# First block: woven projections paced by a running balance over all steps of a phase, and value projections awaited at their first use

## What is computed

```python
proj = h_res @ w_in[l]
(fq, fk, fv, f_logit, sq, sk, sv, c_q, c_kv, k_rot, mq, gate) = split(proj)
out_fox = causal softmax attention(fq, fk, fv, forget gates)         # 4 heads of 64
out_sb  = stick-breaking attention(sq, sk, sv)                       # 4 heads of 64
out_mla = causal softmax attention(rms(c_q) @ w_q_up, rms(c_kv) @ w_kv_up, rope)
out_mem = softmax attention(mq, mem_n @ w_mem_kv[l])                 # 256 memory tokens
y = (concat(out_fox, out_sb, out_mla, out_mem) * silu(gate)) @ w_out[l]
h_res = layer_norm(ALPHA * h_res + y)
```

## Time and profile before

| | us |
|---|---|
| median of 3 runs (2819.11 to 2820.87) | 2819.47 |
| the profiled execution | 2825.36 |
| its span in the trace | 2823.5 |
| TensorE busy | 2645.2 |
| VectorE busy | 1071.4 |
| ScalarE busy | 697.2 |
| first block, layer 0, fox to mem | 136 to 376 |
| first block, layer 1, fox to mem | 545 to 785 |

### The profile page before, as it was taken

The page is one execution under the profiler, slowest core; times in us unless marked ns, Lnnn a source line. Parts: engine busy times, 40 slices in busy tenths (PEclk is TensorE's granted clock), DMA queues, the critical chain, the costliest instruction groups (busy, mean ns, idle before and its releaser), DMA issues. The chain is left out here.

```text
span 2823.5 us, 43376 instructions
## 1 busy us (share of the span) xinstructions
PE 2645.2 (94%) x17418; PEld 1388.3 (49%) x17418; DVE 1071.4 (38%) x2323; ACT 697.2 (25%) x1835; POOL 207.0 (7%) x253
## 2 busy tenths in 40 slices
PE   7999999999999989999999999988999989999897
PEld 3565654565645667555444444435765543322222
DVE  3023340023345854556112112245852552332234
ACT  2124321134322344422112111112442320000000
POOL 1100020000001001012100000001010010000000
PEclk9999999999999999999999999998999999999999
DMA  7243635343714001015999999981012249999996
GB/s 228 75 125 93 161 94 142 99 121 80 212 28 117 31 15 44 32 75 213 368 397 401 397 397 399 381 227 31 16 29 90 97 165 397 404 410 410 403 415 257
DMA packets 268622, 569.97 MB, mean 202 GB/s; under 512 B 12416, under 2 KB 203200, under 8 KB 219328
## 3 DMA queue, kind: packets, MB, share of 16 engines
q1 hardware_dynamic: 256512, 528.69, 51.3%
q0 software_dynamic: 11824, 39.18, 5.1%
q10 hardware_dynamic: 144, 0.14, 0.0%
HBM read 551.53 MB, written 16.42 MB: 201 GB/s over the span
## 5 line engine op out<-in xcount | busy, mean ns | idle before, releaser
L510 PE MATMUL ps<-turned,ring 128*128 128x512 f32 (+1 forms) x1056 | 406.6, 545 | 3.7 <-ACT turned L1745 3.0
L510 PEld LDWEIGHTS ps<-turned,ring 128*128 128x128 f32 x1056 | 201.8, 192 | 202.7 <-issue 191.0
L798 PE MATMUL ps<-ring,mixT 128*128 128x512 f32 x512 | 223.6, 594 | 0.8 <-DVE mixT L1961 0.8
L1391 ACT ACTIVATE work<-ps 128x512 f32<-128x512 f32 x32 | 19.1, 598 | 682.3 <-PE ps L1293 404.5
L2002 ACT ACTIVATE probsT<-ps 128x512 f32<-128x512 f32 (+3 forms) x280 | 120.2, 455 | 230.1 <-PE ps L626 145.7
L1935 DVE TENSOR_REDUCE col<-ps 128x1 f32<-128x256 f32 (+4 forms) x136 | 79.0, 581 | 257.6 <-PE ps L584 224.6
L584 PE MATMUL ps<-kz,qz 96*128 96x512 f32 (+3 forms) x320 | 134.9, 504 | 23.7 <-ACT probs_v L1989 10.8
L1989 ACT ACTIVATE probs_v<-ps,col 128x256 f32<-128x256 f32 (+5 forms) x216 | 136.3, 631 | 81.6 <-DVE col L1935 57.0
L533 PE MATMUL ps<-turned,ring 128*128 128x512 f32 (+1 forms) x352 | 154.6, 568 | 0.9 <-DMA ring<-in_w_in 0.9
L798 PEld LDWEIGHTS ps<-ring,mixT 128*128 128x128 f32 x512 | 95.9, 190 | 114.5 <-issue 113.2
L612 PE MATMUL ps<-const,probs_v 128*128 128x128 f32 x752 | 122.8, 281 | 17.1 <-DVE probs_v L1953 14.1
(11 more groups left out here) (325 smaller groups left out, 3844.7 us busy)
## 6 DMA issues: line engine op xcount, KB each, us to landing
ring<-in_w_gate SPq DMA_DIRECT2D x64, 1024.0 KB, 21.0
mixT<-in_w_up SPq DMA_DIRECT2D x64, 1024.0 KB, 15.0
ring<-in_w_mod SPq DMA_DIRECT2D x96, 512.0 KB, 5.5
ring<-in_w_up SPq DMA_DIRECT2D x48, 1024.0 KB, 20.9
ring<-in_w_in SPq DMA_DIRECT2D x82, 512.0 KB, 7.2
turned<-in_w_gate SPq DMA_DIRECT2D x32, 1024.0 KB, 19.3
mixcT<-in_w_down SPq DMA_DIRECT2D x32, 1024.0 KB, 17.6
probs_v<-in_w_down SPq DMA_DIRECT2D x32, 1024.0 KB, 18.5
```

The lines of the kernel that those rows point to most:

```text
L510: mm = nc.tensor.matmul(ps[:, b, 0:n], w[:, k, :], rhs[:, k, 0:n], start=(k == 0), stop=(k == KD - 1))
L798: mm = nc.tensor.matmul(ps[:, b, :], lhs[:, k, tl * P:(tl + 1) * P], w, start=(k == 0), stop=(k == KD - 1))
```

## The change

Three things. (1) `weave` keeps a balance: what a call leaves or overdraws is carried into the next (a saving up to one more call's budget, a debt in full), and the budgets fall from 2700, 3000 and 1900 a step to 2100, 2400 and 1450. (2) A bank taken by any job, not by woven ones alone, is known to `bank_free` with the step in which it was taken. (3) The waits for the evacuation of the last value projection (sv, mv, memv) move from the start of the phase that uses them to its first value product.

```diff
--- before.py
+++ after.py
@@ -295,6 +295,7 @@
                 pe.wait_ge(*emptied(bank_user[b]))
             bank_user[b] = job
             places[("job", job)] = b
+            closing[job] = now[0]
             return b
 
         def pe_busy(pe, n):
@@ -319,6 +320,7 @@
 
         closed = {}
         closing = {}
+        now = [(None, 0)]
 
         def bank_free(fill):
 
@@ -340,6 +342,7 @@
         def weave(fill, ph, step, budget):
 
             fill["place"] = (ph, step)
+            budget += min(fill["credit"], budget)
             while fill["left"] and step >= fill["not_before"] and budget > 0:
                 said = next(fill["products"], None)
                 if said is None:
@@ -348,9 +351,10 @@
                     fill["not_before"] = max(fill["not_before"], said[1])
                 else:
                     budget -= said[1]
+            fill["credit"] = budget
 
         def filling(products):
-            fill = {"left": True, "not_before": 0, "place": None}
+            fill = {"left": True, "not_before": 0, "place": None, "credit": 0}
             fill["products"] = products(fill)
             return fill
 
@@ -627,11 +631,12 @@
                                           probsT[:, seq[w] % 2, j, :], start=(j == 0), stop=(j == n - 1))
             mm.then_inc(*done("job_done", job))
 
-        def pe_softmax(pe, ph, products=None, budget=0):
+        def pe_softmax(pe, ph, products=None, budget=0, values=None):
             us = joined(ph)
             lag = lag_of(ph)
             fill = filling(products) if products else None
             for i in range(len(us) + lag + 1):
+                now[0] = (ph, i)
                 if i < len(us):
                     pe_scores(pe, us[i])
                 if fill:
@@ -639,6 +644,9 @@
                 if lag <= i < len(us) + lag:
                     pe_turn(pe, us[i - lag])
                 if i > lag and us[i - lag - 1][2] % 2:
+                    if values:
+                        pe.wait_ge(*emptied(values))
+                        values = None
                     pe_pv(pe, us[i - lag - 1])
                 if mods_at(ph, i, 0):
                     pe_mod(pe, mods_at(ph, i, 0))
@@ -657,6 +665,7 @@
 
             fill = filling(products)
             for n in range(4 * HEADS + 2):
+                now[0] = (("sb", l), n)
                 if n < 4 * HEADS:
                     hh, i = sb_unit(n)
                     w = SEQ - i * P
@@ -682,6 +691,7 @@
                         job = ("sbpv", l, hh // 2)
                         b = open_job(pe, job)
                         pe.wait_ge(*at("sb_weights", (l, m)))
+                        pe.wait_ge(*emptied(("sv", l, 1)))
                         for j in range(4):
                             for e in range(2):
                                 mm = nc.tensor.matmul(ps[e * HD:(e + 1) * HD, b, j * P:SEQ],
@@ -879,9 +889,8 @@
                 for c in range(2):
                     yield from n_products(pe, fill, ("sv", l, c), w1(l, "sv", c), hT, NT)
 
-            pe_softmax(pe, ("fox", l, 0), stick_inputs, 2700)
+            pe_softmax(pe, ("fox", l, 0), stick_inputs, 2100)
             pe.wait_ge(*emptied(("sk", l, 1)))
-            pe.wait_ge(*emptied(("sv", l, 1)))
             pe.wait_ge(*at("spare_zeroed", 0))
             narrow_jobs(pe, (4, 5, 6, 7))
 
@@ -952,11 +961,10 @@
                     close_job(job, fill["place"])
                     yield "ns", 860
 
-            pe_stick(pe, l, latent_inputs, 3000)
+            pe_stick(pe, l, latent_inputs, 2400)
             pe.wait_ge(*at("kr_spread", l))
             pe.wait_ge(*at("mla_q", (l, HEADS - 1)))
             pe.wait_ge(*emptied(("mk", l, HEADS - 1)))
-            pe.wait_ge(*emptied(("mv", l, 1)))
             narrow_jobs(pe, (3, 6, 7))
 
             def memory_inputs(fill):
@@ -967,11 +975,10 @@
                 for c in range(2):
                     yield from n_products(pe, fill, ("memv", l, c), w1(l, "mv", c), hcT, NC)
 
-            pe_softmax(pe, ("mla", l, 0), memory_inputs, 1900)
+            pe_softmax(pe, ("mla", l, 0), memory_inputs, 1450, values=("mv", l, 1))
             pe.wait_ge(*emptied(("memk", l, 1)))
-            pe.wait_ge(*emptied(("memv", l, 1)))
             narrow_jobs(pe, (3, 6, 7))
-            pe_softmax(pe, ("mem", l, 0))
+            pe_softmax(pe, ("mem", l, 0), values=("memv", l, 1))
             wide_jobs()
 
             pe.wait_ge(*emptied(("pv", ("mem", l, 0), NT - 1, 1)))
```

## The result

The changed kernel takes 2834.24 us (median of 5 runs, 2831.43 to 2836.66) against 2819.11 for the kernel before (2811.0 to 2820.87): a ratio of 1.0055, 95% interval 1.004 to 1.007. It is slower by about 15 us, 11 to 20 by the interval. The forecast was 2828.7, in a range of 2820 to 2837.

A forecast was written before the change was run, and what follows sets the result against it. With TensorE busy 94% of the span, time in the first block could come only from gaps between its matmuls and its clock. Gaps +5.8 and clock +3.4 made +9.2 us on the median 2819.47: 2828.7 us, range 2820 to 2837.

The forecast's parts named there:

- Fox and mla tails: Ends of fox and mla: waits of 0.26, 0.53 and 0.78 us for turned probabilities go, -3.1 us a layer.
- The load wait: Start of sb: TensorE waits for the cq 0 load, queued behind one waiting for sv 1's last matmul, +5.4 us a layer.
- T: End of the fox phase's last matmul; cq 0 was forecast to land at T + 5.9 us.
- the 4 to 5.5 us named as the sign: Before sb's second matmul group: a DMA wait of this size in both layers would show the forecast right.
- (a): Sb step 11: the first query product waits 2.9 us for DVE's step 10, against 2.8 before; counted as even.
- (b): Late sb: three query heads' rotations in one DVE step make TensorE wait 2.1 us, before 0.2; +1.9 us a layer.
- Start of mla: Before mla's first score: the copy now waited for ends sooner than the DVE pair before, -0.4 us a layer.
- my walk: Fox loop followed step by step with its debts: step 3 bare, sv 1 closing in the final sweep.
- Sum of gaps: Both layers: the gap terms add to +2.9 us a layer, +5.8 us in all.
- The clock: First block: 20 us at half clock, 7 more than before, costing +3.4 us, bounds 0 and +10.
- only the load wait: Rival: load wait at sb's start, nothing inside sb, no extra half clock; +1.0 us a layer, 2821.5 us, chance 0.20.
- The load is hidden: Rival: sv ends by step 17, so only removed gaps count; -4.4 us a layer, 2810.7 us, chance 0.12.

The follow-up runs named there:

- e1: Kernel after with only fox paced by the balance, sb and mla on the old weave and budgets, moved waits kept: 2831.4 us, ratio 1.0046 to the kernel before.
- e4: Kernel after with the two cq loads and the ckv load one conditioning group earlier: 2818.9 us, ratio 1.0001 to the kernel before.
- e11: Kernel after, unaltered, measured and profiled once more: 2833.6 us, ratio 1.0054 to the kernel before.
- e8: Kernel before with only the moved waits for the last value projection, old weave, budgets and load order: 2820.6 us, ratio 1.0010.
- e9: Kernel before with nine extra unread 512-column products (7.8 us) ahead of layer 1's gate products: 2830.0 us, ratio 1.0035.
- e5: Kernel after with sb woven as before (3000 a step, no balance) and cq and ckv loads one conditioning group earlier: 2811.0 us, ratio 0.9964 to the kernel before.

## Why the prediction was right, and where it was off

The sign, the main term and the range held; the rise was 15 us where 9.2 were forecast. By its own steps:

- **Fox and mla tails, -3.1 a layer: right.** All six waits of each layer are gone; the two lines of turned probabilities fell by 5.2 + 1.0 = 6.2 us over both layers. The end of mla in the kernel after, bare of brackets:

```profile
353.48 1.06 PE L551 MATMUL ps<-ring,turned 128*128 128x128 f32 x8
354.46 1.09 PE L630 MATMUL ps<-probsT,probs_v 128*64 128x128 f32 x16
```

- **The load wait, +5.4 a layer: right, 5.6 and 5.9.** Each link shows: the issue 0.03 us after the last sv matmul, cq 0 0.41 us behind it, a landing of 5.3. e1 has it alone, e4 removes it by the order alone. The landing came where the prediction had it (with T at 207.78, T + 5.9 is 213.68, the first product on it starts at 213.62); TensorE asked for it 0.2 us after T and not 0.5, which is why the wait lies just above the 4 to 5.5 us named as the sign. The estimate from the page "DMA: Bandwidth & Descriptors" of the Trainium skill (section "Anatomy of one DMA"), a wait of 3.9 us, comes out too low for these loads from SP. Three issued back to back landed after 4.0, 5.3 and 6.6 us: one more load cost 1.3 us, near the 1.2 that the page's rate gives, but the first took 0.8 us more than its formula.
- **(a) The first query product, 2.9 against 2.8 before: under-sized.** It waited 3.55 us, +0.8 a layer net. The chain was the one named; DVE's end of it, in the kernel after:

```profile
262.00 0.56 DVE L2192 SCALAR_TENSOR_TENSOR work<-ps,work 128x384 f32<-128x384 f32 x1 [5.08 <-ACT work L2162]
262.60 0.54 DVE L2195 TENSOR_TENSOR work<-work,const 128x128 f32<-128x128 f32 x1
263.06 0.69 DVE L2202 TENSOR_TENSOR work<-work,const 128x128 f32<-128x128 f32 x1
...
264.27 1.40 DVE L2238 SCALAR_TENSOR_TENSOR probs_v<-probs_v,vec 128x512 f32<-128x512 f32 x2
```

The two 128-column operations took 0.54 and 0.69 us where I had put 0.3 each from the earlier trace rows; that is the 0.6 that was missing (the terms of the prediction add to 5.0 us rather than its 4.9). Both run beside a copy on POOL:

```profile
261.27 2.34 POOL L2692 COPY kz<-work 32x512 f32<-32x512 f32 x4 [7.57 <-PE ps L921]
```

This repeats in both layers of all thirteen profiles: the two such operations that overlap this copy took 0.40 to 0.54 and 0.69 us, and every other one of the sb phases 0.28 to 0.30. In the kernel before they were the ones at 250.32 and 250.66, beside the copy at 248.88. No run moves the copy away, so that it is the cause is not tested.
- **(b) The bunched rotations, +1.9 a layer: right mechanism, +1.3.** The wait was 1.69 and 1.32 us instead of 2.1. DVE's chain took 12.4 us, near the 12.0 said; TensorE's own work beside it 10.8 (280.28 to 291.09), not 9.9: I had summed bare durations, and from start to start the nine groups took up to 0.3 us more each, 0.9 in all.
- **Start of mla, -0.4: -0.3** (2.0 us to 1.4 over both layers).
- **Missed: 0.49 us in fox step 4, both layers.** The timeline after shows it, where the kernel before had none:

```profile
150.58 2.84 PE L537 MATMUL ps<-turned,ring 128*128 128x512 f32 x6 [0.49 <-ACT modrow L2078]
```

I had step 3 bare in my walk, and costed it at nothing. With it empty, step 4 opens its bank before ACT has emptied the conditioning product of step 2.
- **Sum of gaps, +5.8: +8.7 measured** (28.8 to 37.5). By the waits: tails -6.2, loads and the 0.4 in front of them +9.8, (a) +1.6, (b) +2.6, mla -0.6, fox step 4 +1.0, together +8.2. The largest differences are (a), +1.6 where the sum had nothing, and the missed wait, +1.0; the load wait adds 0.8, mla 0.2, and (b) takes off 1.2.
- **The clock, +3.4: the length was right, the cost nearer 2.** I had put 20 us of the two layers at 1.2 GHz. The kernel after has 20.4, the kernel before 13.6. But only matmuls lose time there, half of what they take, and the stretches that begin in a load wait are partly idle. Here they are, the first two of the kernel after, the last two of e11 (PEclk 0.50):

```profile
210.80:217.60 6.80, 3.98 (x12) 1.43 (x16) 0.00 (x0) 0.00 (x0) 0.00 (x0) 0.50 1.19 296
623.80:630.60 6.80, 3.52 (x4) 1.18 (x4) 0.00 (x0) 0.00 (x0) 0.00 (x0) 0.50 1.19 299
```

```profile
210.10:216.90 6.80, 3.42 (x4) 1.17 (x4) 0.00 (x0) 0.00 (x0) 0.00 (x0) 0.50 1.19 300
626.50:633.30 6.80, 5.24 (x36) 2.59 (x40) 0.00 (x0) 0.00 (x0) 0.00 (x0) 0.50 1.02 247
```

So the two load waits cost 3.8 us of clock in after (half of 3.98 + 3.52) and 4.3 in e11. The other stretches lie in sb and differ from profile to profile, for one kernel too: 3.4 us at 265.4 in after, 6.8 at 264.7 in e11. In all, TensorE worked 13.4 us at 1.2 GHz in after and 18.2 in e11, and 12.9, 9.5 and 12.7 us in before, e8 and e9, which have the weave and the load order of before: some 4 us more, a cost of 2. Their matmuls took 619.6 and 621.9 us against 620.3, 618.6 and 620.1, 1 us more in the mean; in the profiled pair of before and after the cost does not show at all. The seven profiles with another weave or order and no long wait have 613.8 to 617.2; whether the higher figure of before, e8 and e9 is chance or belongs to their weave is not shown.

What of the 15 us do the profiles hold? The stretch from 136 us on takes 657.1 and 659.1 us in after and e11, against 649.1, 647.8 and 649.2 in before, e8 and e9 (without its added products): 9.4 more. From there to the end of the span it is 2041.7 and 2037.1 against 2038.4, 2035.5 and 2036.5: 2.6 more, where two profiles of the same kernel differ by 4.6. That makes 12, inside the interval of 11 to 20; where the rest is, if there is any, stays open. The rival "only the load wait" falls, since (a) and (b) came too. "The load is hidden" would have needed sv 1 to close in step 17. e4 hides the load but keeps (a) and (b) and only equals the kernel before; e5, with sb's weave as before, came to 2811.0, which is what that rival gives.

## What to carry to other kernels

When work is moved later to fill idle steps, follow the buffers that it reads, not only its results: here the later last use of sv 1's slot delayed the load twelve places on, and the cq loads queued behind that one. Spread such work only up to the point where the next phase's first load is still issued one landing time (5.3 and 5.7 us for cq 0 here) before its use, or move that load forward in the order; e5 did the latter, kept sb as it was, and took 0.36% off. And price a long idle wait of TensorE above its length: the two waits of 5.6 and 5.9 us cost about 2 us more each in work at 1.2 GHz.

## What the runs showed of the hardware

- Two profiles of the same kernel have 13.4 and 18.2 us of TensorE's work at 1.2 GHz in the same stretch, and 619.6 and 621.9 us for the same 4026 matmul records. One profile cannot size a clock effect of a few microseconds.
- Six products that nothing reads, put into each of the two idle waits, made the kernel about 6 us faster than the same waits left idle: PEclk was 1.00 in the 19 us in which the idle kernel had 0.83.
- A 128x128 DVE operation on two SBUF tensors took 0.28 to 0.30 us everywhere in sb, except beside POOL's copies of 32x512 into `kz`, where it took 0.40 to 0.69 us, in all thirteen profiles.
